# Half of the low halves of two projections on GpSimd, and 14 gathered rows moved beside them

## Time and profile before

| | |
|---|---|
| median of 3 runs | 2936.31 us (2927.91 to 2942.86) |
| profiled execution | 2944.16 us, span 2942.4 us |
| TensorE (PE) busy | 2783.8 us, 95% |
| VectorE (DVE) busy | 2177.9 us, 74% |
| GpSimd (POOL) busy | 1495.7 us, 51% |
| ScalarE (ACT) busy | 1254.9 us, 43% |
| low halves on GpSimd / VectorE | 207 / 193 |
| bytes moved | 949.47 MB, mean 323 GB/s |

### The profile page before, as it was taken

One profiled execution on the slowest core, in us unless ns is written; L12 is line 12 of the kernel. 1 busy time (PEld: TensorE's weight loads), 2 busy tenths in 40 slices (PEclk: granted clock), 3 DMA queues, 4 the chain that ended last, 5 costly groups with the idle time before them and its releaser, 6 DMA issues.

```text
span 2942.4 us, 43256 instructions
## 1 busy us (share of the span) xinstructions
PE 2783.8 (95%) x17757; PEld 2624.9 (89%) x17757; DVE 2177.9 (74%) x2882; ACT 1254.9 (43%) x1690; POOL 1495.7 (51%) x661
## 2 busy tenths in 40 slices
PE   8899999978989999999999999999999989999988
PEld 6687888856869999999998999999998989999987
DVE  7866637766677788989994777776677767777776
ACT  7656533347233333357773433333333332333331
POOL 0100253222232478862224888887776766676661
PEclk9999999989999999999999999999999999999999
DMA  9757548854887879989999999999999999999985
GB/s 377 268 182 277 213 170 337 328 195 171 304 344 279 339 286 340 336 326 379 358 367 376 370 365 362 380 378 358 354 370 362 369 340 352 380 357 354 394 308 201
DMA packets 188847, 949.47 MB, mean 323 GB/s; under 512 B 17713, under 2 KB 77153, under 8 KB 78913
## 3 DMA queue, kind: packets, MB, share of 16 engines
q1 hardware_dynamic: 116064, 485.54, 44.4%
q0 software_dynamic: 60848, 440.59, 38.4%
q10 hardware_dynamic: 11808, 21.70, 2.1%
HBM read 906.46 MB, written 41.22 MB: 322 GB/s over the span
## 4 chain that ended last, share of the span: by engine, by line
PE 66%; DMA 12%; DVE 10%; ACT 6%; POOL 3%; issue 2%; SPq 0%; ACTq 0%; DVEq 0%
PE ps L1784 12%; PE ps L2132 7%; PE ps L2134 7%; PE ps L2133 7%; PE ps L2064 7%; PE ps L2065 7%; PE ps L2063 7%; DVE ring_lo L1172 5%; DMA ring_raw<-peer_v 4%; PE ps L2048 4%; PE ps L1771 3%; DMA g_in<-gelu_scratch 3%; POOL ring_lo L653 3%; ACT ring_hi L734 2%; PE ps L2106 2%
## 5 line engine op out<-in xcount | busy, mean ns | idle before, releaser
L653 POOL TENSOR_TENSOR ring_lo<-ring_raw,ring_hi 128x2048 fp32r<-128x2048 f32 x207 | 963.4, 4654 | 551.8 <-ACT ring_hi L734 549.8
L734 ACT ACTIVATE ring_hi<-ring_raw 128x2048 fp32r<-128x2048 f32 x396 | 754.4, 1917 | 651.9 <-DMA ring_raw<-peer_u 188.4
L2132 PE MATMUL ps<-a_hi,ring_hi 128*128 128x304 f32 x2048 | 634.2, 310 | 62.7 <-DVE ring_lo L1172 26.4
L2134 PE MATMUL ps<-a_hi,ring_lo 128*128 128x304 f32 x2048 | 626.9, 306 | 0.0
L2133 PE MATMUL ps<-a_lo,ring_hi 128*128 128x304 f32 x2048 | 624.1, 305 | 0.0
L2063 PE MATMUL ps<-bT_hi,ring_hi 128*128 128x304 f32 x2048 | 620.0, 303 | 3.6 <-DVE small L1578 2.5
L2064 PE MATMUL ps<-bT_lo,ring_hi 128*128 128x304 f32 x2048 | 615.6, 301 | 0.0
L2065 PE MATMUL ps<-bT_hi,ring_lo 128*128 128x304 f32 x2048 | 615.5, 301 | 0.0
L1172 DVE TENSOR_TENSOR ring_lo<-ring_raw,ring_hi 128x2048 fp32r<-128x2048 f32 x193 | 483.3, 2521 | 159.7 <-ACT ring_hi L734 159.7
L2132 PEld LDWEIGHTS ps<-a_hi,ring_hi 128*128 128x128 f32 x2048 | 393.6, 192 | 72.1 <-issue 59.3
L688 POOL DMA_INDIRECT rows<-peer_u_rows,idx_far x128 | 201.6, 1575 | 429.9 <-DVE z_far L1420 380.0
(11 more groups left out here) (322 smaller groups left out, 3764.9 us busy)
## 6 DMA issues: line engine op xcount, KB each, us to landing
ring_raw<-peer_u SPq DMA_DIRECT2D x128, 1024.0 KB
ring_raw<-peer_v SPq DMA_DIRECT2D x128, 1024.0 KB
ring_raw<-w_in SPq DMA_DIRECT2D x80, 1024.0 KB
ring_raw<-w_out SPq DMA_DIRECT2D x32, 1024.0 KB
ring_raw<-w_query SPq DMA_DIRECT2D x32, 1024.0 KB
g_quad<-gates_scratch SPq DMA_DIRECT2D x32, 640.0 KB
gelu_scratch<-ahead ACTq DMA_DIRECT2D x72, 152.0 KB
g_in<-gelu_scratch SPq DMA_DIRECT2D x72, 152.0 KB
```

Of the source, the lines that this page charges most:

```text
L653: pool.tensor_tensor(ring_lo[s][:], ring_raw[s][:], ring_hi[s][:].bitcast(F32), ALU.subtract)\
L734: act.activation(ring_hi[place(n)][:], ring_raw[place(n)][:], ACT.Copy).then_inc(hi_ok[SLOT[n]], 1)
L2132: pe.matmul(dst, hi[:, col], a_hi[:, par, e, :], start=(e == 0), stop=False)
L2134: last = pe.matmul(dst, lo[:, col], a_hi[:, par, e, :], start=False, stop=(e == GROUP - 1))
```

## The change

In pieces 114 to 141, the odd pieces' low halves (14 of them) are made by GpSimd. Each of these odd pieces gets one gathered row more on VectorE. As the number of rows is fixed, the stretch of pieces 284 to 395 gets 144 rows instead of 158. GpSimd's walk through the pieces starts at piece 112 instead of 144, with the same lag of three pieces.

```
 def lo_on_pool(n):
+    if OUT_B + 2 <= n < AHEAD - 2:
+        return n % 2 == 1
     if n in POOL_A or DOWN <= n < BOTH or AHEAD <= n < AHEAD + HOT_FIRST:
         return True
...
     for n in range(OUT_B, AHEAD - 1):
         ROWS_AT[n] = 0 if n == QUERY_B - 1 else 1 if n == QUERY_B - 2 or n % 4 == 3 and n < QUERY_B else 2
+        if OUT_B + 2 <= n < AHEAD - 2 and n % 2 == 1:
+            ROWS_AT[n] += 1
...
             pool.wait_ge(far_sel, 2)
             pool.wait_ge(h_far_made, 1)
-            gather_freed_before(AHEAD - ROW_LAG)
-            for n in range(AHEAD, N_PIECES):
+            gather_freed_before(OUT_B - ROW_LAG)
+            for n in range(OUT_B, N_PIECES):
                 if lo_on_pool(n):
                     make_lo(n)
                 gather_freed_before(n + 1 - gather_lag(n))
```

## The result

The kernel after takes 2976.88 us (median of four runs, 2969.97 to 2980.89). The kernel before took 2932.76 beside it (2927.91 to 2942.86). The ratio is 1.0153, interval 1.0117 to 1.0190: 1.5% slower. The prediction was 2934, range 2907 to 2970; the time lies outside the range.

A forecast was written before the change was run, and what follows sets the result against it. TensorE, busy 95% of the span, was taken as the bound. Middle +39 and last stretch -41, with 0 between, sum to -2; put on the 2936.3 us median this gave 2934, range 2907 to 2970.

The forecast's parts named there:

- The last stretch: Final expert pieces: 14 rows less, 273.9 MB at the average rate, take 761 us, a gain of 41.
- small return: Rival, chance 0.27: middle costs +45 or more, last stretch returns only 16, its waits being single late transfers and the lock; 2965.
- The middle: Output and query projections of tiles 1 to 3: queue order +38, port about +1, together +39 us.
- VectorE's even low halves, 2 to 6 us each: Sign: TensorE would wait this long for them between 741 and 1080 us.
- The order of GpSimd's queue: Middle: a two-piece chain of low half, gather, landing and rows takes 18.9 or 21.1 us, outpacing TensorE; +38.
- The port: Middle: VectorE operations with two SBUF inputs block beside GpSimd's low halves; +13, less 12 for quicker landings, leaving +1.
- g: Chain term in the middle: gather and landing of a row, 8.7 us at the median, 7.03 to 11.05 as bounds.
- some 60 us more: Middle: extra cost compared with no lock if none of the 14 blocks of 4.6 us were hidden.
- about level: Middle stages: VectorE's own sum hardly changes, 14 rows replacing 14 low halves of 2.29 us each.
- the 0.4 us edge: Middle before the change: TensorE's 0.4 us wait for a low half, read as VectorE's slack used up in places.
- The clock: Middle: stalls of 5 us bring 0.46 us matmuls, 2.5 us more a pair, staying just inside the chain's steps.
- +66 to +90: Middle's upper bound: g of 11.05 with the port's waits in full; its upper end was not believed.

The follow-up runs named there:

- e8: Kernel after with only seven rows moved, to odd pieces 129 to 141 (query projection), VectorE making all middle low halves and GpSimd gathering freely; 2914.6 us.
- e3: Kernel after with a lag of two pieces instead of three in pieces 112 to 141; 2936.4 us.
- e5: Kernel after with a lag of two pieces and the rows of pieces 112 to 143 reduced from one SBUF input, without the h_far product; 2906.7 us.
- e2: Kernel after with the 14 rows moved, but VectorE making all middle low halves and GpSimd gathering there without a loop over its pieces; 2917.3 us.
- e7: As e2, but VectorE works on 1024 of 2048 columns of the middle's rows, with all loads kept; 2903.3 us.

## Why the prediction was wrong

**The last stretch: right in size.** Without moved rows the expert part is 1825.3, 1816.6, 1808.8 and 1806.4, mean 1814.3. With all 14 moved it is 1779.2, 1773.3, 1768.1, 1775.3, 1770.9, 1777.8 and 1766.1, mean 1773.0. The difference is 41.3; the forecast was 41, by fewer bytes at the average rate. The stretch itself is 754.8, at 364 GB/s, near TensorE's floor of 748.2. That its waits were single late transfers which 5% fewer bytes would leave ("small return") is refuted. Whether it was the bytes stays open. The 14 rows also took 32 us of VectorE's work with them, 20.8 of the 37.1 us of waits were for VectorE, and no run takes only the one or the other away. That seven rows gained 33.0 (e8, one trace) speaks against a price by the byte alone.

**The middle: +39 forecast, 88.6 measured.** The query stage began at 946.9 instead of 919, the expert pieces 89.8 us later than before instead of 35 to 45. "VectorE's even low halves, 2 to 6 us each" were waited for up to 8.2, the norm behind them up to 18.8 where it was 10.4 before, and squares up to 7.9.

**The order of GpSimd's queue: right in kind.** Low half, gather, landing, rows, gather, low half is the chain of every second step in the output stage, and loosening it is worth 37.5 to 39.7. That the forecast's 38 lies so near is in part luck. The 38 holds a gather of 2.75 in every step, 1.8 of which is already a wait for VectorE. The measured steps are 3.5 and 3.3 longer than the forecast's. The ways through ScalarE and through TensorE's next load are not in it. The lag edit leaves part of the order and takes some block along.

**The port: this step failed.** The prediction put it at "+13" less "12", on the ground that "Most of these 4.6 us fall inside g, where VectorE has 9 to 11 us of other work in a 17 us gap". It measured 32.2 and 30.0, for the rows and the gathers alone. In six steps of six GpSimd starts its low half within 2 us before VectorE starts a row. In three of them the row is the one whose buffer the next gather needs. In the other three the delay falls on GpSimd's own low half and the gather right behind it. In the query stage it falls on VectorE's low half, for which TensorE waits. None of these lies inside g. The waits of gathers, 2.75 at most once a step in the sum, stand on the chain twice (806.50 and 822.34), and g stood for one gather where two are in line. At lag 2 the block is felt in GpSimd's queue: TensorE's waits for its low halves are 27.5 us with it (e3) and 13.7 without (e5). The other side was seen and set aside: the prediction had "some 60 us more" for no cover at all, and half of that came. The Trainium skill, SBUF — State Buffer, "Who interferes with whom", says that such a block lasts for the whole instruction of the winner; 6.65 against 2.29 beside a low half of 4.86 agrees. The rule was used for the price of one block; it should have been asked of each instruction on the chain whether it can meet a low half.

**The rows themselves: a second step that failed.** VectorE's own sum was called "about level", so it was taken to cost nothing that 14 rows replace 14 low halves, and their landings were priced only inside the chain. But rows come where the 0.4 us edge had shown no slack: alone they cost 28.3 (e2), about half of it VectorE's time (e7). With low halves moved in exchange, at lag 2 and without the block of rows, 18.9 are left (e5), of which the waits are for GpSimd's low halves. What the exchange would cost with no order at all no run shows.

**The clock** was named as a second way to the slow side, with 2.5 us a pair, and judged to stay inside the steps. In sum 27.0 of the 88.6 are matmuls at a lower clock. It isn't a cause of its own: with TensorE's idle time down from 79.1 to 30.2 us (e5) the clock is 0.97 again. Each of the three terms above carries its share of it.

**The range** ended at 2970 because the upper end of the bound of +66 to +90 for the middle was not believed, for the reason that blocks and landings overlap. With that bound kept and -41, the total would have read up to 2985 and held the time.

## What to carry to other kernels

When work goes to an engine with an in-order queue that also issues transfers, price the loop from its make to the transfer to the consumer and back, and compare it with the bottleneck's pace; where it is longer, the position of the transfer in the queue is an edit of its own (here 38 us for one piece less of lag). For a shared port, ask of each instruction on that loop whether it runs just when the other engine does: a block is hidden only if nobody waits for the blocked instruction. Moving rows from a stretch with DMA at 0.94 to one at 0.84 and 0.81 returned here the 41 us that the bytes had forecast (whether by the bytes is not shown). But half the rows in the stage with the longer pace, left in their engine's free-running queue, kept more than all of them with the work moved as well.

## What the runs showed of the hardware

- A gather's issue on GpSimd took 0.94 to 0.96 us alone. It took 2.75 to 2.84 where some 2 us of a VectorE operation with two SBUF inputs were still to come, and 1.88 to 1.91 where it was some 1.1 us (784.28, 809.57). The one at 783.02, which began 0.04 us behind such a row, took 0.96, and the row 2.36. Beside VectorE's additions, with one input in PSUM, it took 0.94 (793.21). Over 67 gathers the mean was 1652 ns with such rows and 1168 with rows of one SBUF input. It is the gather that waits: VectorE's low half beside the one at 817.95 took 2.28, its usual time.
- GpSimd's low half loses by it too: 5.80 at 825.12 where 4.6 is usual, 5068 against 4640 ns in the mean.
- VectorE's low halves lose as well: 7.13 and 7.14 at 1004.44 and 1055.11, beside a low half of GpSimd, for 2.29 elsewhere.
- Gathers did not land sooner where less was moved: the median from issue to landing was 8.9 us in the middle of after, at 273 GB/s (5.5 to 12.5), and 8.8 in that of e2, at 321 (6.8 to 14.1).
